# Twelve modulation vectors of a two-block network: five summed on TensorE in column groups, seven on VectorE, and no weight splits on GpSimd

## The reference

```
c_act = jax.nn.silu(c)
for i in range(DEPTH_2):                                  # 2 layers
    mod = (c_act @ mod_w[i] + mod_b[i]).reshape(B, 6, D)[:, :, None, :]
    hin = x * (1.0 + mod[:, 1]) + mod[:, 0]
    y = mla_mixer(...) if i == 0 else moba_mixer(...)     # attention, 8 heads
    x = layer_norm(DEEPNORM_ALPHA * x + mod[:, 2] * y, ln_g[i, 0], ln_b[i, 0])
    hin = x * (1.0 + mod[:, 4]) + mod[:, 3]
    y = conv_ffn(hin, ...)                                # 1024 -> 2 x 2816 -> 1024, gelu
    x = layer_norm(DEEPNORM_ALPHA * x + mod[:, 5] * y, ln_g[i, 1], ln_b[i, 1])
```

## Time and profile before

| what | us |
|---|---|
| time, median of 3 runs | 995.38 |
| lowest and highest of them | 994.42, 997.2 |
| the profiled execution | 995.37 |
| its span, first to last instruction | 993.5 |
| PE busy | 895.3 |
| DVE busy | 765.0 |
| ACT busy | 511.3 |
| POOL busy | 357.2 |

### The profile page before, as it was taken

The page is one execution under the profiler, slowest core; times in us unless marked ns, Lnnn a source line. Parts: engine busy times, 40 slices in busy tenths (PEclk is TensorE's granted clock), DMA queues, the critical chain, the costliest instruction groups (busy, mean ns, idle before and its releaser), DMA issues.

```text
span 993.5 us, 14234 instructions
## 1 busy us (share of the span) xinstructions
PE 895.3 (90%) x5536; PEld 779.5 (78%) x5536; DVE 765.0 (77%) x1045; ACT 511.3 (51%) x781; POOL 357.2 (36%) x164
## 2 busy tenths in 40 slices
PE   5989989999977898978899999978998889999994
PEld 4978868666865786768799999867986778999993
DVE  4697887598797787779888889889697797555555
ACT  5664554555554644446465555553654465454540
POOL 0450222122050443105432425259151178342425
PEclk9999999999998997989899999979998899999997
DMA  8785643554765473237778878737664277665601
GB/s 278 284 267 186 215 168 109 165 187 146 261 216 169 170 245 123 79 110 275 255 273 276 315 252 284 291 104 272 213 218 148 67 274 274 214 231 167 206 32 43
DMA packets 56188, 200.19 MB, mean 201 GB/s; under 512 B 6412, under 2 KB 7348, under 8 KB 56120
## 3 DMA queue, kind: packets, MB, share of 16 engines
q1 hardware_dynamic: 55816, 198.21, 58.2%
q0 software_dynamic: 304, 1.06, 0.3%
HBM read 198.18 MB, written 1.06 MB: 201 GB/s over the span
## 4 chain that ended last, share of the span: by engine, by line
PE 62%; DVE 25%; issue 5%; ACT 5%; POOL 3%; DMA 0%; POOLq 0%; DVEq 0%; ACTq 0%
PE ps L974 19%; PE ps L975 18%; PE ps L976 18%; DVE wsp L1180 6%; PE ps L1129 3%; DVE acc L1239 3%; PE ps L1150 1%; ACT wsp L1712 1%; DVE X L1604 1%; DVE arena L1341 1%; DVE ra L1180 1%; DVE pb L1458 1%; DVE arena L1168 1%; DVE wk L1216 1%; PE ps L1136 1%
## 5 line engine op out<-in xcount | busy, mean ns | idle before, releaser
L974 PE MATMUL ps<-XT,wsp 128*128 128x256 f32 x768 | 219.7, 286 | 9.1 <-DVE wsp L1180 6.8
L975 PE MATMUL ps<-XT,wsp 128*128 128x256 f32 x768 | 216.2, 282 | 0.0
L976 PE MATMUL ps<-XT,wsp 128*128 128x256 f32 x768 | 216.1, 281 | 0.0
L974 PEld LDWEIGHTS ps<-XT,wsp 128*128 128x128 f32 x768 | 146.7, 191 | 13.0 <-DVE wsp L1180 9.5
L1180 DVE TENSOR_TENSOR wsp<-ring,wsp 128x1024 fp32r<-128x1024 f32 x90 | 144.5, 1610 | 11.4 <-ACT wsp L1712 11.3
L975 PEld LDWEIGHTS ps<-XT,wsp 128*128 128x128 f32 x768 | 146.6, 191 | 0.9
L976 PEld LDWEIGHTS ps<-XT,wsp 128*128 128x128 f32 x768 | 146.7, 191 | 0.0
L1712 ACT CAST wsp<-ring 128x1024 fp32r<-128x1024 f32 x116 | 121.0, 1047 | 48.7 <-PE ps L976 41.6
L1180 DVE TENSOR_TENSOR wsp<-arena,wsp 128x1024 fp32r<-128x1024 f32 (+1 forms) x81 | 128.3, 1587 | 11.2 <-ACT wsp L1712 11.2
L2012 POOL TENSOR_TENSOR wsp<-ring,wsp 128x1024 fp32r<-128x1024 f32 x26 | 69.8, 2683 | 147.3 <-ACT wsp L1712 147.3
L1712 ACT CAST wsp<-arena 128x1024 fp32r<-128x1024 f32 (+1 forms) x92 | 95.7, 1043 | 30.2 <-PE ps L976 30.0
(11 more groups left out here) (265 smaller groups left out, 1982.6 us busy)
## 6 DMA issues: line engine op xcount, KB each, us to landing
ring<-in_mod_w SPq DMA_DIRECT2D x64, 512.0 KB, 4.4
arena<-in_mod_w SPq DMA_DIRECT2D x32, 512.0 KB, 4.5
arena<-in_ffn_o SPq DMA_DIRECT2D x25, 512.0 KB, 4.6
ring<-in_ffn_a SPq DMA_DIRECT2D x23, 512.0 KB, 4.7
arena<-in_ffn_b SPq DMA_DIRECT2D x23, 512.0 KB, 4.8
ring<-in_ffn_b SPq DMA_DIRECT2D x21, 512.0 KB, 4.8
arena<-in_ffn_a SPq DMA_DIRECT2D x21, 512.0 KB, 4.7
ring<-in_ffn_o SPq DMA_DIRECT2D x19, 512.0 KB, 4.6
```

The source lines that it names most:

```text
L974: pe.matmul(o, l[0], r[0], start=start, stop=False)
L975: pe.matmul(o, l[0], r[1], start=False, stop=False)
L976: return pe.matmul(o, l[1], r[0], start=False, stop=stop)
```

## The change

- `modulation()` is written anew. The vectors are numbered n = 0 to 11. Loads are issued one step ahead (`soon`).
- Vectors 0 to 4 go to PE. `cact` is kept 32 times side by side in a new tile `cactr`. For a block k, four fp32 matmuls put 32 columns of `cactr` against 256 columns each of the loaded block; the j-th writes partitions 32j to 32j + 31 of one PSUM bank, which adds up over the eight blocks. ACT copies the bank to `msum` (`mod_sum`). For a column vector PE then transposes the two halves of `msum` (`mod_pe`), for a row vector it spreads one row over all partitions with a matmul against a column of the identity.
- Vectors 5 to 11 are summed on DVE alone, all eight blocks (`mod_v`), in one of two accumulators `acc`, which now lie in the arena and are free from the end of the first layer's attention on (`mla_end`). PE adds up the partitions in fp32: two matmuls of 512 columns for a row, eight of one column for a column vector (`mod_pv`).
- The steps `mr_hi` and `mr_lo`, the scaling on ACT and the additions on GpSimd are gone.
- `POOL_PART` is 0 in all stages: GpSimd makes no low part.
- The ring has seven slots. `MOD_PACE` is lower in the stages up to the end of the first attention and in the second layer.

```diff
-MOD_PACE = [0.7, 0.9, 0.8, 1.25, 1.0, 0.8, 0.65]
+MOD_PACE = [0.52, 0.52, 0.52, 0.52, 0.76, 0.32, 0.5]
-POOL_PART = [0.1, 0.5, 0.15, 0.2, 0, 0.3]
-LAG, DELAY = 1, 2
+POOL_PART = [0, 0, 0, 0, 0, 0]
+LAG = 1
-    bank, raw, part, wk = Turn(8), Turn(5), Turn(4), Turn(3)
+    bank, raw, part, wk = Turn(8), Turn(7), Turn(4), Turn(3)
...
     def modulation():
+        sums = [None, None]
+        soon = [load(("mod_w", 0))]
+        for n in range(12):
+            i, m = n // 6, n % 6
+            if n < 5:
+                b = bank.get()
+            elif n == 5:
+                while mla_end is None:
+                    yield
+                sums = [mla_end, mla_end]
+            for k in range(8):
+                s = soon.pop(0)
+                if n * 8 + k + 1 < 96:
+                    soon.append(load(("mod_w", n * 8 + k + 1)))
+                if n < 5:
+                    add("mod_k", i, m, k, s, b, prior("bank", b))
+                else:
+                    add("mod_v", i, m, k, s, sums[n % 2])
+                free_raw(s)
                 yield
+            if n < 5:
+                add("mod_sum", i, m, b, sums[n % 2])
+                bank.put(b[0])
+            yield
...
+                elif kind == "mod_k":
+                    i, m, k, s, b, before = a
+                    for e in new("P", ("ld", *s), ("cact", 1), before):
+                        pe.wait_ge(*e)
+                    for j in range(4):
+                        ins = pe.matmul(ps[b[0]][32 * j:32 * j + 32, 0:256], cactr[:, k * 32:(k + 1) * 32],
+                                        raw[s[0]][:, j * 256:(j + 1) * 256], start=k == 0, stop=k == 7,
+                                        tile_position=(0, 32 * j))
+                    ins.then_inc(*done("P", "mod_k", i, m, k, also=[("raw", *s)]))
...
                     if br is not None:
-                        pe.matmul(ps[b[0]], ones_r[:, :], mr[:, 0:512], start=True, stop=False)
-                        ins = pe.matmul(ps[b[0]], ones_r[:, :], mr[:, 512:1024], start=False, stop=True)
+                        for j in (2 * cb, 2 * cb + 1):
+                            ins = pe.matmul(ps[b[0]][:, (j % 2) * 256:(j % 2) * 256 + 256],
+                                            bass.AP(cst, 32 * j, [[NCONST, 128], [0, 128]]), total, start=True, stop=True)
                     else:
...
+                        for k in range(2):
+                            ins = pe.transpose(ps[b[0]][:, k * 128:(k + 1) * 128], total[:, k * 128:(k + 1) * 128], ID)
...
+                elif kind == "mod_pv":
+                    i, m, cb, b, before, br = a
+                    total = acc[m % 2]
+                    for e in new("P", ("mod_v", i, m, 7), ("cst",), before):
+                        pe.wait_ge(*e)
+                    if br is not None:
+                        ins = pe.matmul(ps[b[0]], ones[:, 0:128], total[:, cb * 512:(cb + 1) * 512], start=True, stop=True)
+                    else:
+                        for k in range(8):
+                            ins = pe.matmul(ps[b[0]][:, k:k + 1], total[:, k * 128:(k + 1) * 128], ones[:, 0:1],
+                                            start=True, stop=True)
...
+                elif kind == "mod_v":
                     i, m, k, s, before = a
+                    x = acc[m % 2]
...
                     if k == 0:
-                        ins = ve.tensor_scalar(acc[0], raw[s[0]], cact[:, 0:1], None, MUL)
+                        ins = ve.tensor_scalar(x, raw[s[0]], cactr[:, 0:1], None, MUL)
                     else:
-                        ins = ve.scalar_tensor_tensor(acc[0], raw[s[0]], cact[:, k:k + 1], acc[0], MUL, ADD)
+                        ins = ve.scalar_tensor_tensor(x, raw[s[0]], cactr[:, 32 * k:32 * k + 1], x, MUL, ADD)
...
+                elif kind == "mod_sum":
+                    i, m, b, before = a
+                    for e in new("A", ("mod_k", i, m, 7), before):
+                        ac.wait_ge(*e)
+                    ac.copy(msum[m % 2], ps[b[0]][:, 0:256]).then_inc(*done("A", "mod_sum", i, m, also=[("bank", *b)]))
...
-                    po.tensor_tensor(acc[1], acc[1], raw[s[0]], ADD).then_inc(
-                        *done("G", "mod_b", i, m, k, also=[("raw", *s)]))
...
-                    po.tensor_tensor(acc[0], acc[0], acc[1], ADD).then_inc(*done("G", "mod_sum", i, m))
```

More of the change, by code:

```diff
@@ L306, in modulation @@
     def modulation():
[L307 to L313, removed]
-                    yield
-                add("mod_sum", i, m)
-                yield
[L317 to L336, removed]
-                yield
@@ new lines, in modulation @@
+        sums = [None, None]
[6 more added lines that the diff above has]
+                while mla_end is None:
+                    yield
+                sums = [mla_end, mla_end]
[8 more added lines that the diff above has]
+                free_raw(s)
+                yield
+            if n < 5:
+                add("mod_sum", i, m, b, sums[n % 2])
+                bank.put(b[0])
+            yield
+            is_row, r = m in (2, 5), 0 if m == 2 else 1
+            while i and is_row and ("r2", r) not in have:
+                yield
+            br = load(("row", "mod_b", i * 6144 + m * 1024)) if is_row else None
+            if is_row:
+                yield
+            for cb in range(2 if is_row else 1):
+                b = bank.get()
+                add("mod_pe" if n < 5 else "mod_pv", i, m, cb, b, prior("bank", b), br)
+                sums[n % 2] = ("mod_pe", i, m, cb)
+                bank.put(b[0])
+            if is_row:
+                free_raw(br)
+            else:
+                add("mod_fin", i, m)
+            have.add(("mod", i, m))
+            yield
@@ L339, in order @@
+    mla_end = None
     mod = W.beside(modulation(), MOD_PACE[0])
@@ L785, in grid @@
             return ap.rearrange("p (k n) -> p k n", k=k)
-        ring_t = sb("ring", 5120)
+        ring_t = sb("ring", 7168)
         wsp = sb("wsp", 8192, f32r)
@@ L795, in build @@
         R2 = sb("R2", 2048)[:, :].rearrange("p (m n) -> p m n", m=2)
-        acc = [sb(f"acc{i}", 1024)[:, :] for i in range(2)]
+        cactr = sb("cactr", 256)[:, :]
+        msum = [sb(f"msum{i}", 256)[:, :] for i in range(2)]
         small = sb("small", 512)
-        arena = sb("arena", 14864)
+        arena = sb("arena", 14866)
         ra = sb("ra", 8192, f32r)
@@ L842, in build @@
         ARr, FS, BC, MR, NM = (scr[0:4, 1536 + i * 256:1792 + i * 256] for i in range(5))
+        acc = [arena[:, 12818:13842], arena[:, 13842:14866]]
         cosT, sinT, posf = scr[:, 0:256], scr[:, 256:512], scr[:, 512:770]
@@ L851, in build @@
         vv = grid(arena[:, 6400:8448], 2)
-        raw = [ring_t[:, i * 1024:(i + 1) * 1024] for i in range(5)]
+        raw = [ring_t[:, i * 1024:(i + 1) * 1024] for i in range(7)]
         raw += [GTf[:, 0:1024], GTf[:, 1024:2048], mvf[:, 0:1024], mvf[:, 1024:2048], avf, cqf, qrf]
@@ L1266, in vector @@
                     a_, s_ = MC[i][:, x:x + 8], MC[i][:, x - 8:x]
-                    for e in new("V", ("mod_ev", i, m, 1)):
+                    for e in new("V", ("mod_ev", i, m, 0)):
                         ve.wait_ge(*e)
```

64 lines of the change are left out of this document (16 added, 48 removed).

## The result

The changed kernel takes **966.97 us** (median of four runs, 965.84 to 967.2), the kernel before 996.19 us beside it (994.42 to 997.2): a ratio of 0.969, 95% interval 0.967 to 0.972. I had forecast 988 us; the time lies inside the range and on the forecast side, but the gain is 29 us where I had 7. It is near the time of the first rival, 964 us, in which the four column groups overlap fully. The profiled execution took 967.04 us with a span of 965.3, and its mean granted clock is 0.976 (0.955 before).

A forecast was written before the change was run, and what follows sets the result against it. PE, the fullest engine, was taken to wait mainly for DVE, held up by GpSimd's 1024 wide operations. 995.4 − 51 (gain) − 3 (small work on PE) + 47 (five vectors on PE) = 988 us, range 957 to 1012.

The forecast's parts named there:

- the first rival: mod_k on PE: the four column groups overlap fully, 23 us in place of 47, total 964 us; chance 0.27.
- the five vectors on PE: Cost of 40 mod_k steps of four fp32 matmuls on PE: 51 us, 47 after some 4 in existing waits.
- between them: passes start in the order of the program: Middle case for mod_k: each further group adds one pass, 1.28 us a step, 51 us; chance 0.45.
- The two bounds: mod_k step on PE: full overlap of four groups 0.63 us (25 us in all), no overlap 1.92 us (77 us).
- the way out: Leaving the column groups after a mod_k step: taken equal to the way in, 0.10 us, together 0.2 a step.
- The gain: PE time won by relieving GpSimd: 36 us of waits, 9 of clock, 6 of short holes; 51 us, range 36 to 66.
- the clock: PE's slow stretches after waits: 21.12 us of work at half the clock lose 10.6 us; 9 us taken as gain.
- holes too short for the list: PE holes of about 0.1 us hidden by overlapping matmuls: 6 us gain, by no row, bounds 0 and 12.
- the marks that I had set for a wrong gain: Sign in the profile after: gain wrong if PE's waits without ACT's still add up to 30 us.
- The chains beside the feed-forward: Seven vectors' DVE chains, nearly all in the first feed-forward: costed at nothing while DVE gets under some 17 us late.
- The loads: PE waiting for mod_k's loads, issued one step ahead: costed at 0 with seven ring slots, bound 10 us.
- The third rival: Holes stay as PE waits for ACT's casts or mod_k's loads: 1005 us, or 1013 with half missing; chance 0.10.

The follow-up runs named there:

- e8_half: The changed kernel with each column group's 256 columns in mod_k done as two matmuls of 128 columns next to each other; 968.46 us.
- e1_one_group: The changed kernel with the four matmuls of a mod_k step sent to one column group for k = 1 to 7 (35 of 40 steps); 1011.40 us.
- e12_two_columns: The changed kernel with mod_k's four matmuls replaced by one of 2 columns over the whole array for k = 1 to 7; 948.80 us.
- e6_before_dve: The kernel before with every modulation vector's eight steps as one DVE chain, none on ACT and GpSimd, weight splits and mr kept; 965.74 us.
- e5_before_nosplit: The kernel before with no weight splits on GpSimd, the modulation as it was; 978.39 us.
- e10_before_both: The kernel before with no weight splits on GpSimd and all modulation steps as DVE chains, none on ACT and GpSimd; 952.89 us.
- e2_pool_splits: The changed kernel with the shares of weight splits that GpSimd had before put back; 974.23 us.
- e4_dve12: The changed kernel with all twelve vectors as DVE chains, none on PE's column groups, and five ring slots; 955.03 us.
- e3_ring5: The changed kernel with five ring slots, as before, instead of seven; 966.83 us.

## Why the prediction was wrong, point by point

**The term that failed: the five vectors on PE.** The forecast put 51 us, less 4 absorbed, on the step "between them: passes start in the order of the program", 1.28 us for mod_k. It costs 0.76: the overlap is full. The order that I took doesn't hold: in the changed kernel the first passes of the four groups start within 0.02 us, and in e8_half a later group's matmul starts before an earlier group's second one. My reason was that in every row the two passes of a matmul stand next to each other. Those rows were all of matmuls over the whole array, or of one group alone, and say nothing on two groups. The two bounds, 0.63 and 1.92, stood for the right cases, and e1_one_group shows the upper one: 0.76 + 1.27 = 2.03 us. Both lie 0.11 to 0.13 us under what was measured, by the second error below. With nothing to choose between bounds 52 us apart, the middle was no safer than either end; the timeline of the changed kernel decides at a glance, but no row before the change could.

**A second error in the same term: the way out.** I took 0.10 us for the way into a narrower part of the array, by a row, and the same for the way out, by none. The row's own surroundings had the price; this is what follows L1150 in the kernel before:

```profile
214.35 0.65 PE L1150 MATMUL ps<-pt,arena 128*64 128x128 f32 x4
214.93 0.50 PE L974 MATMUL ps<-wsp,XT 128*128 128x512 f32 x1
215.26 0.39 PE L975 MATMUL ps<-wsp,XT 128*128 128x512 f32 x1
```

From L1136's start at 214.04 to 215.26 it would be 0.89 us at the distances of full-width neighbours (six passes of 128 columns 0.109 apart, one matmul of 512 columns 0.234), and it is 1.22: 0.33 us for both ways, as in mod_k, where I took 0.2. That is 5 us over 40 steps. The 4 us that I let vanish in other waits did not vanish (e12_two_columns).

That the first rival's time lies 3 us from the result is in part luck: it had a price of 23 us and a gain of 51, and measured are 30 and 55.

**The gain.** I took 51 us, range 36 to 66. By the sum it was 995.4 + 30 − 3 − 967.0 = 55 us (the 3 us of smaller sums on PE were not measured apart). Of the waits that I had listed:

| PE's wait | before | after | gain | forecast |
|---|---|---|---|---|
| low halves of DVE (wsp) | 18.4 | 4.3 | 14.1 | 14.5 |
| low halves of GpSimd | 6.0 | 0 | 6.0 | 5.5 |
| mr | 4.6 | 0 | 4.6 | 4.6 |
| softmax step | 8.8 | 1.6 | 7.2 | 5.5 |
| ACT, layer norms | 10.3 | 10.2 | 0.1 | 0 |

That is 32 us in the lines that I could name and 30 in the forecast. With its other lines the list of waits falls from 82.7 to 44.5 us, so waits gave 38 us, where I had 36. The other 17 us of the 55 stand against 15 in the forecast, 9 for the clock and 6 for holes too short for the list. They are the clock, as far as the traces tell. Summed over the stretches at a granted clock of 0.50, the level of 1.2 GHz, in which PE still works, the kernel before (twelve stretches) and the changed one (four) show:

```profile
sum 78.52, PE 62.45 PEld 51.64 DVE 57.46 ACT 34.23 POOL 17.00; mean PE 5.20 PEld 4.30 DVE 4.79 ACT 2.85 POOL 1.42
```
```profile
sum 34.15, PE 25.38 PEld 21.59 DVE 22.99 ACT 20.11 POOL 6.22; mean PE 6.34 PEld 5.40 DVE 5.75 ACT 5.03 POOL 1.56
```

Half of the 37 us of PE's work that left the low clock is 18.5 us, by estimate. My 9 us came from five of the twelve stretches; for the 6 us, laid by no row, nothing is left. That the gain of 55 us came out near the 51 is in part luck: the clock was put at half its size, and a term without a row made good for it.

Of the marks that I had set for a wrong gain, one was reached: PE's waits without ACT's add up to 34 us, where 30 were to mean that the gain had failed. The mark was badly laid, since 15 of them (L1221 and DVE's layer norms, L1626 and L1674) were there in the same size before.

**The mechanism** of the gain held: GpSimd's 1024 wide work made DVE late, and DVE made PE late. e6_before_dve, e5_before_nosplit and e10_before_both show it without PE's column groups: 31, 19 and 45 us, the first and the last with ACT's copies gone too. One reading of mine in it was off: the L1239 of 3.43 us ended before the first of the three additions was half done; it stood beside a weight split of GpSimd (L2012, 286.14 to 289.57 us), so that hole had both kinds of GpSimd's work in it. In the changed kernel the splits are worth only 7 us (e2_pool_splits), and 4.2 of these are one wait for GpSimd's own low half. That DVE has more room there, as five vectors no longer need it in the first 440 us, fits; this was argued, not tried.

**The chains beside the feed-forward** cost next to nothing, as forecast: no wait of PE in 480 to 620 us, and one of 1.5 us at 620.71, for a step of GpSimd (L2105) that took 3.9 us while DVE did chain steps and low halves. **The loads** of mod_k cost nothing, with seven slots or with five. **The third rival**, holes that stay, fell: PE's waits without ACT's and without those that were there in the same size before (L1221, the layer norms of DVE) are short.

**What the change could have been.** e10_before_both differs from the changed kernel above all in the five vectors: chains on DVE instead of column groups. It is 14 us faster. e4_dve12 differs from the changed kernel in these vectors and in the ring, which is worth nothing (e3_ring5), and is 12 us faster. The groups cost PE 30 us, so a DVE freed of 40 steps gives back some 16 to 18 of them; that is the difference, not measured by itself. The forecast never asked whether PE, the fullest engine, should get these vectors at all. Its own working had the hint, since the chains on DVE beside the feed-forward stood in it at nothing.

## What to carry to other kernels

Ask first which engine holds up the critical one, and take the work off that engine's neighbour, before moving any work onto the critical engine. Here the two moves in one change were worth −45 us (e10_before_both) and, by the difference to it, +14, and only the first was needed. Where two bounds of an unknown price lie far apart, say which single row would decide, and don't take the middle for caution. A price that has a way in and a way out is read over both, from the last neighbour before to the second one after. A chain that is slowed down to give an engine room has a floor, the time at which its result is read; below it the whole rest comes in one burst.

## What the runs showed of the hardware

- Four fp32 matmuls in four column groups take the time of one: two passes for all, 0.43 us for 256 columns in each. A further step right behind it adds just these 0.43 us; the way in and out costs 0.33 us together, seen in the starts of the neighbours, and as much where a matmul 64 columns wide stands between full-width ones. In one group the same work takes 1.27 us more.
- What one column group has queued doesn't hold back another, though its matmuls stand earlier in the program: 16 passes of 128 columns merged to 0.66 us, 8 passes of 256 to 0.64, and the 16 start in four sets of four (e8_half).
- The contention between DVE and GpSimd works both ways. The 512 wide step that stays on GpSimd got slower as DVE got more two-input work, from 1740 ns in the mean to 2106. The longest took 6.2 us, at 806.56, and beside it DVE did a chain step and four low halves one right behind the other, at their usual 1.28 and 1.22 us. PE waited for such a step only 1.5 us, once. The group in the changed kernel (busy us, mean ns, idle before), and its line (ns min/median/max):

```profile
L2105 POOL TENSOR_TENSOR ra<-wk,ra 128x512 fp32r<-128x512 f32 x22 | 46.3, 2106 | 282.2 <-ACT ra L2019 282.2
```
```profile
L2105 POOL TENSOR_TENSOR ra<-wk,ra x22: 1297/1591/6155, 450.6 to 940.9; 128x512 fp32r<-128x512 f32 x22
```
